# First two expert blocks gathered from rank-made lists, routing work moved into the last tile and into the first expert run, in a one-core hybrid decoder layer

## The reference, cut to what matters

```python
h = x + hybrid_mixer(rms_norm(x, attn_norm), ...)          # (1024, 1024)
xt = rms_norm(h, ffn_norm)
pg = softmax(xt @ w_rg); pg_top, grp = top_k(pg, 1)         # 4 groups
el_sel = (xt @ w_re).reshape(t, 4, 8)[grp]
top_p, top_i = top_k(softmax(el_sel), 2); top_p /= sum(top_p)
expert = grp * 8 + top_i                                   # 32 experts, 2048 assignments
y[token] += weight * ((silu(x @ w_gate[e]) * (x @ w_up[e])) @ w_down[e])
out = rms_norm(h + y, final_norm)
```

## Time and profile before

| | |
|---|---|
| median of 3 runs | 1507.29 us (1506.79 to 1509.23) |
| the profiled execution's own time | 1509.35 us |
| its span, first to last instruction | 1507.8 us |
| PE busy, share of the span | 1400.4 us, 93% |
| DVE busy | 684.2 us, 45% |
| mean granted TensorE clock | 0.967 |
| DMA moved | 402.20 MB, mean 267 GB/s |

### The profile page before, as it was taken

The page is one execution under the profiler, slowest core; times in us unless marked ns, Lnnn a source line. Parts: engine busy times, 40 slices in busy tenths (PEclk is TensorE's granted clock), DMA queues, the critical chain, the costliest instruction groups (busy, mean ns, idle before and its releaser), DMA issues.

```text
span 1507.8 us, 37606 instructions
## 1 busy us (share of the span) xinstructions
PE 1400.4 (93%) x15106; PEld 847.5 (56%) x15106; DVE 684.2 (45%) x1947; ACT 462.8 (31%) x1311; POOL 246.8 (16%) x319
## 2 busy tenths in 40 slices
PE   6999999999999999999997839999999999999984
PEld 3565665665655656656655515555555555555541
DVE  1483773873855747738738771112111121111206
ACT  2742732824626427328236100001010010100102
POOL 0000100001001001000000021433334334344320
PEclk9999999999999999999998758999999999999997
DMA  8954745545546447456454057999999999999867
GB/s 348 384 205 166 261 155 184 203 172 194 192 160 228 151 167 255 152 181 218 170 178 161 4 217 286 414 405 405 402 401 403 394 393 397 386 402 400 338 234 303
DMA packets 57391, 402.20 MB, mean 267 GB/s; under 512 B 10377, under 2 KB 10569, under 8 KB 35441
## 3 DMA queue, kind: packets, MB, share of 16 engines
q1 hardware_dynamic: 42224, 363.72, 63.2%
q0 software_dynamic: 15104, 37.80, 6.7%
HBM read 380.87 MB, written 29.36 MB: 272 GB/s over the span
## 4 chain that ended last, share of the span: by engine, by line
PE 79%; DVE 11%; ACT 4%; issue 3%; DMA 3%; POOL 0%; DVEq 0%; SPq 0%; POOLq 0%; ACTq 0%
PE ps L550 24%; PE ps L787 22%; PE ps L808 11%; DVE big L1121 5%; PE duo L706 3%; PE ps L706 3%; PE ps L486 2%; DMA big<-in_w_in 2%; PE ps L662 2%; PE duo L774 1%; PE duo L512 1%; PE duo L504 1%; ACT xin L933 1%; PE duo L798 1%; ACT big L940 1%
## 5 line engine op out<-in xcount | busy, mean ns | idle before, releaser
L787 PE MATMUL ps<-big 128*32 128x256 f32 x6144 | 340.1, 381 | 2.1 <-DVE big L1121 2.1
L787 PEld LDWEIGHTS ps<-big 128*32 128x32 f32 x6144 | 197.9, 110 | 134.5 <-issue 7.6
L550 PE MATMUL ps<-big,xin 128*128 128x386 f32 (+1 forms) x672 | 270.2, 539 | 1.0 <-DMA big<-in_w_in 1.0
L550 PE MATMUL ps<-big 128*128 128x512 f32 (+2 forms) x608 | 211.2, 499 | 13.9 <-DMA big<-in_w_in 13.9
L1121 DVE TENSOR_TENSOR big<-big 128x256 f32<-128x256 f32 (+5 forms) x293 | 157.6, 560 | 58.7 <-ACT big L899 35.7
L1572 DVE SCALAR_TENSOR_TENSOR big<-big,ps 128x128 f32<-128x128 f32 x96 | 27.1, 283 | 322.3 <-ACT big L1073 322.3
L808 PE MATMUL ps<-big 128*32 128x256 f32 x3072 | 172.4, 380 | 0.9 <-ACT big L1077 0.9
L550 PEld LDWEIGHTS ps<-big,xin 128*128 128x128 f32 x672 | 122.0, 193 | 90.6 <-issue 48.8
L550 PEld LDWEIGHTS ps<-big 128*128 128x128 f32 x608 | 113.2, 192 | 91.9 <-issue 72.0
L808 PEld LDWEIGHTS ps<-big 128*32 128x32 f32 x3072 | 97.3, 110 | 66.1 <-issue 5.0
L1073 ACT ACTIVATE big<-ps 128x128 f32<-128x128 f32 x96 | 26.6, 277 | 336.3 <-PE ps L787 336.3
(11 more groups left out here) (255 smaller groups left out, 1527.0 us busy)
## 6 DMA issues: line engine op xcount, KB each, us to landing
big<-in_w_gu SPq DMA_DIRECT2D x64, 2048.0 KB, 10.1
big<-in_w_in SPq DMA_DIRECT2D x64, 1024.0 KB, 4.6
big<-in_w_down SPq DMA_DIRECT2D x32, 2048.0 KB, 10.4
big<-in_w_in SPq DMA_DIRECT2D x64, 772.0 KB, 4.4
big<-in_w_in SPq DMA_DIRECT2D x32, 512.0 KB, 4.3
hn_rows<-big POOLq DMA_DIRECT2D x8, 1024.0 KB, 7.0
big<-y_rows SPq DMA_DIRECT2D x8, 1024.0 KB, 11.9
big<-in_x SPq DMA_DIRECT2D x8, 512.0 KB, 10.1
```

The costliest lines, as they stand in the source:

```text
L550: last = t_.matmul(ps[6 + n % 2][:, 0:w], x_src[:, k, :], wv[:, k % KH, :], start=k == 0, stop=k == KD - 1)
L787: last = t_.matmul(ps[GU[t]][TG * j:TG * (j + 1), 0:2 * HC], xT[:, k, TG * t:TG * (t + 1)], wgu[par][k // KH][:, :, k % KH, HC * j:HC * (j ...
```

## The change: what it does

- **Picks.** `pick_experts` is split. `pick_groups` and `pick_first` for seven tiles run right after the rotary work of the last tile, `pick_second` after its second convolution, `count_before` where `pick_groups` was. Their buffers now alias `xin` and `rtab`, which are free by then.
- **Ranks.** The ranks of seven tiles are multiplied inside the last tile, between the two halves of the output projection, into bank 7. Of the last tile only its own 32 columns are left for after the mixer.
- **Lists of blocks 0 and 1.** From rank+1 times `cnd`, DVE makes one-hot rows of 96 positions for experts 0 and 1 (`in_first`); PE multiplies them with the token numbers (`first_products`, seven tiles early, one late); DVE turns the sums into row numbers `first_rows`. POOL fetches each block with one indirect DMA of 96 whole rows of 4 KB, into the later `yo` space and into `hbuf`. The transposes are then 8 of 96x128, the gain 2 instructions of 384.
- **Tables.** `in_wgt` and the multiplied `in_grp` go: the token numbers and weights are multiplied into the small `tok_pos` and `wgt_pos`, and one `in_grp` of four wide instructions serves both. Their products (`table_quarters`) stand inside the first gate/up run ahead of its last two of eight k, and one product of 330 columns after it (`tables`) repeats both tables. `wslot`, `slots` and the loads of the loop bounds come after that.
- **Rows.** In the last tile ACT, not DVE, writes `hnb`, after the logits; POOL stores its two copies with two DMAs, and the first gathers wait only for the first copy.

```diff
+NF = 2
@@ PE, mixer, nxt=False, between the halves of the output projection
+                if not nxt:
+                    pe.wait_ge(sem("routed"), 1)
+                    E.wait("proj_copied", i)
+                    rank_products(0, NT - 1)
                 E.wait("mixed", i)
@@ PE, after the mixer
-            t_.matmul(ps[0][:, 0:256], cn("stri"), cnd, start=True, stop=False)
-            t_.matmul(ps[0][:, 0:256], cn("ones"), mrun[:, 0:NT, :], start=False, stop=True)
-            t_.matmul(ps[1][:, 0:32], cn("ones"), mrun[:, NT, :], start=True, stop=True).then_inc(sem("ranks"), 1)
+            pe.wait_ge(sem("dst_ready"), 1)
+            first_products(0, NT - 1, 4)
+            pe.wait_ge(sem("routed"), 3)
+            t_.matmul(ps[1][:, 0:32], cn("ones"), mrun[:, NT, :], start=True, stop=True)
+            rank_products(NT - 1, NT)
+            pe.wait_ge(sem("dst_ready"), 2)
+            first_products(NT - 1, NT, 2)
...
+            def first_products(t0, t1, bank):
+                for e in range(NF):
+                    for t in range(t0, t1):
+                        last = t_.matmul(ps[bank][0:BLK, e:e + 1], in_first[:, e, t, :], tokf[:, t:t + 1],
+                                         start=t == t0, stop=t == t1 - 1)
+                last.then_inc(sem("slots_summed"), 1)
...
-            x_block(0, 0, 0)
+            first_x_block(0, first_tok[0])
             gate_up(0, 0, 0, True)
-            x_block(1, 0, 1)
+            tables()
+            first_x_block(1, first_tok[1])
+            pe.wait_ge(sem("blk_ready"), 1)
...
             h_block(0)
@@ PE, gate_up
-                if first:
-                    pe.wait_ge(sem("wslot_ready"), 1)
                 for k in range(KD):
+                    if first and k == KD - 2:
+                        table_quarters()
@@ ACT, mixer
                 s.activation(lg[:, i, :], ps[5][:, 32:68], ACT.Copy, scale=r2).then_inc(sem("logits"), 1)
+                if not nxt:
+                    s.activation(hnb, hbuf[:, :], ACT.Copy, scale=r2).then_inc(sem("logits"), 1)
@@ DVE, mixer, nxt=False
+                if not nxt:
+                    E.wait("xnT", i)
+                    pick_groups(0, NT - 1)
+                    pick_first(0, NT - 1)
...
                 conv(1)
+                if not nxt:
+                    pick_second(0, NT - 1)
...
                     if l == LEVELS - 1 and not nxt:
-                        pick_groups(0, NT - 1)
+                        count_before()
...
-                    pick_experts(0, NT - 1)
-                    count_before()
...
+                    dve.wait_ge(sem("ranks"), 1)
+                    first_ranks(0, NT - 1)
+                    for e in range(NF):
+                        last = tt(in_first[:, e, 0:NT - 1, :], heads(cn("giota")[:, 1:BLK + 1], NT - 1),
+                                  bc(first_pos[:, 0:NT - 1, e], BLK), ALU.is_equal)
@@ DVE, after the mixer
+            first_ranks(NT - 1, NT)
+            tt(in_first[:, :, NT - 1, :], heads(cn("giota")[:, 1:BLK + 1], NF), bc(first_pos[:, NT - 1, :], BLK),
+               ALU.is_equal).then_inc(sem("dst_ready"), 1)
...
+            dve.wait_ge(sem("slots_summed"), 2)
+            seq(tt(first_sum[0:BLK, :], ps[2][0:BLK, 0:NF], first_sum[0:BLK, :], ALU.add))
...
+            v.tensor_copy(first_rows[0:BLK, :], first_row[0:BLK, :]).then_inc(sem("slots_ready"), 1)
...
+            first_x_gain(0)
...
+            for r in range(4):
+                some = slice(CT * r, CT * r + CT)
+                tt(in_grp[:, some, :], heads(cn("giota"), CT), bc(groupf[:, some], N_GR), ALU.is_equal) \
+                    .then_inc(sem("dst_ready"), 1)
...
+            dve.wait_ge(sem("slots_summed"), 3)
+            v.tensor_copy(quarter_sums, ps[6][:, 0:2 * N_GR]).then_inc(sem("quarters_copied"), 1)
+            dve.wait_ge(sem("slots_summed"), 4)
+            seq(v.tensor_scalar(wslot[:, :], ps[5][:, N_GR:2 * N_GR], 0.5, None, ALU.mult))
...
@@ POOL
-                pool.dma_start(hn_v[i], heads(hnb, 2)).then_inc(sem("hn_stored"), 16)
+                    pool.dma_start(hn_v[i][:, 0, :], hnb).then_inc(sem("hn_stored"), 16)
+                    pool.dma_start(hn_v[i][:, 1, :], hnb).then_inc(sem("tail_stored"), 16)
...
-            gather(0, 0, True)
-            gather(1, 1, True)
+            for e, rows in enumerate(first_tok):
+                g.indirect_dma_start(rows[0:BLK, :], None, hn_d,
+                                     bass.IndirectOffsetOnAxis(ap=first_rows[0:BLK, e:e + 1], axis=0),
+                                     bounds_check=2 * SEQ - 1, oob_is_err=False).then_inc(sem(f"tok_loaded{e}"), 16)
+            pool.wait_ge(sem("slots_ready"), 2)
+            pool.wait_ge(sem("tail_stored"), 16)
```

More of the change, by code:

```diff
@@ L220, in build @@
         rot = part(512)
+        RTAB_AT = used[0]
         rtab = part(128)
@@ L287, in build @@
         blki = part(NB_MAX + 2).bitcast(I32)
+        first_rows = part(NF).bitcast(I32)
+        first_pad, first_row, first_sum = [part(NF) for _ in range(3)]
         used[0] = 0
@@ new lines, in _, with table_quarters @@
+            first_products(0, NT - 1, 4)
[4 more added lines that the diff above has]
+            first_products(NT - 1, NT, 2)
+            def table_quarters():
+                for n, pos in enumerate((tok_pos, wgt_pos)):
+                    for r in range(4):
+                        pe.wait_ge(sem("dst_ready"), 2 + r + 1)
+                        for j in range(CT):
+                            last = t_.matmul(ps[6][TG * j:TG * (j + 1), N_GR * n:N_GR * (n + 1)],
+                                             pos[:, CT * r + j, :], in_grp[:, CT * r + j, :], start=r == 0, stop=r == 3)
@@ L768, in _, with first_x_block @@
-            last_pair = pe.value_load(blki[0:1, NB_MAX + 1:NB_MAX + 2], min_val=NB_MIN // 2 - 1,
-                                      max_val=NB_MAX // 2 - 1)
+            def first_x_block(e, rows):
+                pe.wait_ge(sem(f"tok_loaded{e}"), 16)
+                for k in range(KD):
+                    last = t_.transpose(ps[k // 4][:, (k % 4) * P:(k % 4) * P + BLK], rows[0:BLK, k * P:(k + 1) * P],
+                                        ident[0:BLK, 0:BLK])
+                last.then_inc(sem("xt_done"), 1)
@@ new lines, in first_x_gain @@
+            def first_x_gain(e):
+                dve.wait_ge(sem("xt_done"), e + 1)
+                for half in range(2):
+                    ks = slice(KH * half, KH * half + KH)
+                    last = tt(xT[:, ks, :], b4(half)[:, :, 0:BLK], bc(g2c[:, ks], BLK), ALU.mult)
+                last.then_inc(sem("xT_ready"), 1)
+            first_x_gain(0)
+            dsf = dst[:, :, :].rearrange("p a b -> p (a b)")
+            seq(v.tensor_copy(dsti[:, :, :].rearrange("p a b -> p (a b)"), dsf))
```

190 lines of the change are left out of this document (101 added, 89 removed).

## The result

The changed kernel takes 1506.45 us (median of 22 runs; all but one between 1502.1 and 1510.97). The kernel before, beside it, takes 1509.42 us (22 runs, 1505.64 to 1514.22). The ratio is 0.9978 with a 95% interval from 0.9967 to 0.9988, so 3.3 us less, with 1.8 and 5.0 us as its ends. The forecast was 1499.3 us in 1494 to 1505.

A forecast was written before the change was run, and what follows sets the result against it. PE's time paces the expert blocks, so the second run's start carries the end. First run 13.4 us earlier (last tile +3.0, lists, fetch), 5.4 given back in run and tail: 1507.29 - 8.0 = 1499.3 us, range 1494 to 1505.

The forecast's parts named there:

- Rival D: First run held by `hn_stored` or DVE's order until the tables are done: 5.4 us slower, 1512.7 us; chance 0.02.
- The last tile: Up to the residual sum: 3.0 us later, from 2.3 for the second pick and 0.75 for rank products.
- The lists: From logits to the early token list: 11.5 us earlier, list ready at 883.1.
- The fetch: POOL waits for the first copy, gathers at 886.0, rows land about 891.9; first run starts at 895.0, 13.4 earlier.
- Rival A: Stores land before the list, so the gather goes at 883.2: 5.8 us more gain, 1493.5 us; chance 0.13.
- Rival C: Fetch of 4 KB rows does not spread over 16 engines: 15.5 us instead of 1.0, total 1513.8; chance 0.05.
- The first run: First gate/up run: 11.64 us as before, cold start included, plus 2.25 for table products, ending at 908.9.
- rival B: Table products at half clock in the first run (+3.95) and a cold second run (+1.1): 1504.3 us; chance 0.15.
- The tail: Between first and second gate/up runs: old 3.3 us plus 3.15 new work, a gap of 6.45 us.
- The second run: Second gate/up run: starts at 915.35, 8.0 us earlier; a cold start, 1.1 us, in the range but not the sum.

The follow-up runs named there:

- e10: Changed kernel with the second pick of seven tiles moved into DVE's idle time late in the last tile, counts and rank work moved later; 1506.30 us.
- e8: Changed kernel with expert 1's gate/up weights (4 MB) held until block 1's rows have landed; 1499.05 us.
- c3: e8 plus, inside block 0's gate/up run, quarter products before product 5 and the wide product before product 6; 1494.19 us.
- e4: Changed kernel with `pick_second` moved ahead of `count_before` in the last wait of the triangular solve; 1505.94 us.
- c1: e8 and e10 together, with 5 dummy products ahead of block 0's transposes, 1 behind them and 4 before the second run; 1495.89 us.
- c4: c3 with 5 dummy products ahead of block 0's transposes and 1 behind them; 1496.42 us.
- e1: Changed kernel with four dummy products of 512 columns on PE in the gap before the second gate/up run; 1502.86 us.
- e3: Changed kernel with expert 1's gate/up weights (4 MB) held until all token stores but the second copy have landed; 1504.65 us.
- e5: Changed kernel with positions and masks made during the first fetch, and quarter and wide products before products 4 and 6 of the first run; 1502.84 us.
- c5: c4 with the edit of e10 as well; 1495.38 us.

## Why the prediction was wrong, by its steps

All from T0. The prediction's third run was at 152.5 (940.48 - 8.0 - 779.98), measured 157.13: 4.6 us short. Three terms make these 4.6 up: the clock of the second run, the clock of the first, and the fetch. Rival D (the change does not do what it says) fell: PE waited for nothing but the rows.

- **The last tile: right.** Forecast +3.0 at the residual sum, measured 89.26 against 86.06, +3.2. The pick 2.2 at the forget gate and 2.5 by 66.45 (before 64.03), where 2.3 was said, the rank products 0.75 (four instructions, 861.23 to 861.99) where 0.75 was said. e10 shows the same 2.5 us from the other side, at 63.98.
- **The lists: right in kind, 1.0 us too early.** List at 104.1, forecast 103.1. The logits came 0.45 earlier, not 0.7, since they wait for PE's router product (2.33 us in the chain). The three products of 32 columns took 1.5 us at half clock, not 1.0. None of it counted: POOL waited for the store.
- **The fetch: start of the first run at 116.3, forecast 115.0; 1.3 of the 4.6.** Rival A (stores in before the list) fell: the first copy landed 108.2 after T0, 4 us behind the list; the forecast was 105.9. From there to the rows 5.4 us passed, 1.5 on POOL until the gather starts and 3.90 for the gather; the forecast had 6.0, but made up otherwise: POOL's share lay beneath a wait for the second copy, and the rows themselves were put at 1.0. The second copy landed at 892.0, 1.0 us after the gather started, so that wait was hardly tested. Where both copies were long in (e8, c3), a gather took 4.19 and 3.85: about 4 us is the bare price of 96 rows of 4 KB, and the forecast's 1.0, made from the bandwidth of long loads, was four times too small; the copy's 2.3 us were the miss that counted. Transposes and gain took 0.35 less than said. Rival C (slower, the rows on one engine, 15.5 us) fell with that, and with it the only slower case of weight.
- **The first run: 15.30, forecast 13.9; 1.4 of the 4.6.** The table products took 2.24 (forecast 2.25), so this half of rival B fell. At full clock this run is 7.77 + 2.24 + 2.59 = 12.6 us; its cold start cost 2.7. The forecast had taken over the run before with its own cold start, 11.64 us against 4 x 2.59 = 10.4, so 1.3. That cost is not a constant: 1.5 in e10, 2.1 in c3, 2.9 in e4, 3.0 in e8, and 0.2 to 0.3 in c1 and c4 with their dummies.
- **The tail: right.** 6.49 us from run to run, forecast 6.45; with 1.3 us for DVE's loads of the bounds, where 1.0 was said.
- **The second run: 12.41 instead of 10.57; 1.84 of the 4.6, and the step that failed.** The prediction had seen the row (clock 1.00 behind 3.3 us) and asked what twice the gap would do, and then left the answer out of the sum, at a price of 1.1 taken from one run. e1 shows it cleanly: same gap, same waits, dummies in it, 10.57. All six profiles with this gap have a cold second run, so the term belonged into the sum; its size of 1.8 is this profile's, the six went from 1.2 to 2.0. The Trainium skill ("TensorE: Matmul & The Clock Gate", section "HAM oscillation") says that waits between bursts return the array to its slow clock. This trace agrees with it at 6.4 us and 2.29 busy (0.50 behind it); for 3 us with 1.4 busy the runs went both ways. Followed, it would have put this term into the sum, at the forecast's own price of 1.1.

So the likeliest case should have been the second half of rival B, with a clock cost at both runs. At 1.1 us for each it would have read 1501.5 us from the median, and by the terms above 1499.3 + 4.6 = 1503.9. That rival B as written says 1504.3 is chance: 3.95 of its us are for table products at half clock, and they ran at full. The other 2.1 us up to about 1506 are not the change's: beside it the kernel before came at 1509.42, not at the 1507.29 from which the forecast started.

## What to carry to other kernels

When a change shortens the work around a wait, ask for each stretch behind it at which clock it will run, and put that into the sum: a gap that doubled cost 1.2 to 2.0 us, and a run that follows a half-idle stretch 1.3 to 3.0 us. Give that term a range and not a number; here the same code gave both ends. When a small transfer on the critical path is slow, look at what shares the engines before cutting it: 0.5 MB took 3.5 us without and 11.3 us beside 4 MB of weights that nobody needed for another 48 us; and hold those until the whole chain of small transfers is through, since holding them for the first link (e3) only moved the collision to the next. A piece of work put "into idle time" has to be checked on PE's clock as well: moving the pick and the rank work out of the chain was worth 2.1 us at the residual sum, and in two of three profiles the clock took 1.2 and 1.7 of them; and what the moved work pushes back must be looked for too, here the list. Dummy products that keep the clock up are work as well: in c4 they held PE past the landing of the rows.

## What the runs showed of the hardware that was not expected

- The granted clock is not a function of the program near it. Equal gaps (3.00 us, 1.39 and 1.40 busy) ended at 0.50 in c4 and at 1.00 in c3, e5 and c5 (e5 and c5 had 1.42 and 1.47 busy). In e10 it rose 3 us later than in c1 over the same code up to there (70.5 and 67.3 after T0), and in c1, but not in e10 and c5, it fell behind a wait of 1.86 us. The first run's cold start cost between 1.5 and 3.0 us in changed kernels without dummies. What decides it stays open.
- Between the landing of a store that POOL waits for and the start of its indirect DMA 1.5 us passed (889.53 to 891.01), in the chain as "issue" and POOLq; where the gather waited for DVE's list instead (e8), it was 0.9.
- The 14 products of one column for the early list, 28 instructions, took 4.62 us of PE at half clock (876.11 on); they ended 0.4 us before the last count began, so this cover nearly went too. In c1 and c5, where they start later, it did: their 4.64 us stand on the chain.
